# Neighbourhood attention with the softmax scale applied to the probabilities and the tile pipeline one tile deeper

## What is computed

```python
s_nb = q @ k_band.T * scale + bias          # window of 8 x 16 positions, the rest masked
s_ctx = q @ k_ctx.T * scale
p = softmax(concatenate([s_nb, s_ctx]))     # one softmax over both
o = p[:, :n_band] @ v_band + p[:, n_band:] @ v_ctx
```

## Time and profile before

| | us |
|---|---|
| median of 3 runs (lowest to highest) | 4434.53 (4432.39 to 4434.57) |
| the profiled execution's own time | 4424.82 |
| its span, first to last instruction | 4422.8 |
| mean granted TensorE clock | 0.939 of full |
| PE busy over the span | 3919.2 (89%) |
| attention groups, first scores to last output | 259.3 to 1040.6 |

### The profile page before, as it was taken

The page is one execution under the profiler, slowest core; times in us unless marked ns, Lnnn a source line. Parts: engine busy times, 40 slices in busy tenths (PEclk is TensorE's granted clock), DMA queues, the critical chain, the costliest instruction groups (busy, mean ns, idle before and its releaser), DMA issues. The chain is left out here.

```text
span 4422.8 us, 55661 instructions
## 1 busy us (share of the span) xinstructions
PE 3919.2 (89%) x23164; PEld 2962.6 (67%) x23164; DVE 1172.5 (27%) x3113; ACT 799.4 (18%) x1768; POOL 497.6 (11%) x497
## 2 busy tenths in 40 slices
PE   5599999988949999999966999999988699999994
PEld 0266666664537789999844666666645589997873
DVE  2312222221221011111125555555533201111114
ACT  0123333331100000000012333333321000000001
POOL 0210000001420000000024111111013200000002
PEclk9799999998969999999988999999988799999997
DMA  9670000010155446778952000000102645579995
GB/s 371 185 305 24 19 24 19 19 48 25 43 180 171 134 151 214 247 261 277 311 194 65 14 16 15 15 15 15 44 15 78 206 162 194 193 249 310 311 308 171
DMA packets 469098, 621.06 MB, mean 140 GB/s; under 512 B 27136, under 2 KB 346128, under 8 KB 468728
## 3 DMA queue, kind: packets, MB, share of 16 engines
q1 hardware_dynamic: 440312, 521.58, 35.9%
q0 software_dynamic: 22240, 73.58, 4.6%
q10 hardware_dynamic: 6312, 22.45, 1.3%
HBM read 550.54 MB, written 67.40 MB: 140 GB/s over the span
## 5 line engine op out<-in xcount | busy, mean ns | idle before, releaser
L1610 PE MATMUL ps<-item_xT,expert_ring 128*128 128x128 f32 (+9 forms) x8192 | 1169.4, 306 | 1.1 <-DVE item_xT L1687 1.1
L1610 PEld LDWEIGHTS ps<-item_xT,expert_ring 128*128 128x128 f32 x8192 | 1115.6, 192 | 57.2 <-issue 5.7
L1643 PE MATMUL ps<-item_aT,expert_ring 128*128 128x144 f32 (+8 forms) x2304 | 409.1, 333 | 0.0
L1643 PEld LDWEIGHTS ps<-item_aT,expert_ring 128*128 128x128 f32 x2304 | 359.7, 193 | 25.3 <-issue 2.0
L1694 DVE TENSOR_TENSOR item_aT<-item_silu,ps 128x128 f32<-128x128 f32 (+9 forms) x256 | 83.8, 327 | 1069.2 <-ACT item_silu L1664 1069.2
L1664 ACT ACTIVATE item_silu<-ps 128x128 f32<-128x128 f32 (+9 forms) x256 | 79.1, 309 | 1314.9 <-PE ps L1610 1314.9
L683 PE MATMUL ps<-hT,w_group 128*128 128x512 f32 (+1 forms) x704 | 270.2, 527 | 0.4 <-PEq L301 0.4
L383 PE MATMUL ps<-hT,oT 128*128 128x512 f32 x576 | 254.5, 602 | 1.4 <-PEq L917 0.7
L1009 PE MATMUL ps<-hT,w_group 128*128 128x512 f32 (+1 forms) x576 | 232.4, 546 | 0.4 <-PEq L301 0.4
L1560 POOL DMA_INDIRECT gathered<-h_rows,slot_idx x55 | 52.6, 956 | 1531.2 <-PE ps L1593 1520.3
L1705 DVE COPY item_y<-ps 128x512 f32<-128x512 f32 (+3 forms) x106 | 69.0, 684 | 573.9 <-PE ps L1623 397.0
(11 more groups left out here) (207 smaller groups left out, 4223.5 us busy)
## 6 DMA issues: line engine op xcount, KB each, us to landing
expert_ring<-in_expert_w_gate SPq DMA_DIRECT2D x128, 1024.0 KB, 5.1
expert_ring<-in_expert_w_up SPq DMA_DIRECT2D x128, 1024.0 KB, 8.0
expert_ring<-in_expert_w_down SPq DMA_DIRECT2D x64, 2048.0 KB, 7.7
mod_ring<-in_mod_w SPq DMA_DIRECT2D x24, 2048.0 KB, 14.0
slot_out<-rows POOLq DMA_DIRECT2D x7, 4096.0 KB, 46.3
w_group<-in_w_qkv SPq DMA_DIRECT2D x48, 512.0 KB, 3.7
slot_out<-item_y ACTq DMA_DIRECT2D x35, 512.0 KB, 7.5
h_rows<-hr SPq DMA_DIRECT2D x18, 512.0 KB, 2.6
```

Of the source, the lines that this page charges most:

```text
L1610: m = nc.tensor.matmul(gub(j, b, w), ring[:, b // 2, k, w * 256 + (b % 2) * P:w * 256 + (b % 2 + 1) * P], xT[:, k, 0:C], start=k == 0, sto ...
L1643: m = nc.tensor.matmul(yb(j, d), ring[:, 4 + d // 4, f, (d % 4) * P:(d % 4 + 1) * P], aT[:, f, 0:C], start=f == 0, stop=f == FB - 1)
```

## The change

The probabilities are now scaled by the inverse sums on DVE before they are transposed (`normalised`), in place of a diagonal, a matmul, a copy and a product behind `values`. The scores of a tile are issued two tiles ahead, not one; they wait (`s_pre`) until DVE has read the scores of the tile before out of the score banks. A projection chunk is issued in one piece at the end of a tile's turn. The transposes of the fifth block go to bank 6, beside the values, where they wait for `s_oT`.

```diff
-                FIFTH = bank(4, 0, 2 * P).rearrange("p (h n) -> p h n", h=2)
+                FIFTH = bank(6, P, 3 * P).rearrange("p (h n) -> p h n", h=2)
                 O = bank(6, 0, P)
-                INV = bank(6, P, 2 * P)
...
                     def scores(g, par, i):
                         t = order[i]
                         if i == 0:
                             pe.wait_ge(s_qk, g * NQK + NQK)
+
+                        pe.wait_ge(s_pre, g * 2 * NS + 2 * i)
...
-                    def transposes(g, i):
+                    def transposes(g, i, first=False):
                         n = len(near_keys(order[i]))
-                        if i == 0:
-                            pe.wait_ge(s_v, g * 3 + 3)
                         for h in range(2):
-                            pe.wait_ge(s_exp, g * 2 * NS + 2 * i + h + 1)
+                            pe.wait_ge(s_nm, g * 2 * NS + 2 * i + h + 1)
...
+                        if n > 4:
+                            if not first or i:
+
+                                pe.wait_ge(s_oT, g * NS + i)
...
                     def group(g, par, first=False, last=False):
                         for i in range(NS):
-                            if i + 1 < NS:
-                                scores(g, par, i + 1)
+                            values(g, par, i, first)
+                            if i + 2 < NS:
+                                scores(g, par, i + 2)
                             elif not last:
-                                scores(g + 1, 1 - par, 0)
-                            fifths(g, i)
-                            inverse_rows(g, i, first)
-                            if i < NM and not last:
-                                project(g + 1, i, 0)
-                            values(g, par, i)
-                            if i < NM and not last:
-                                project(g + 1, i, 1)
+                                scores(g + 1, 1 - par, i + 2 - NS)
                             if i + 1 < NS:
                                 transposes(g, i + 1)
                             elif not last:
                                 transposes(g + 1, 0)
+                            if i < NM and not last:
+                                project(g + 1, i)
...
                     scores(0, 0, 0)
-                    transposes(0, 0)
+                    transposes(0, 0, True)
+                    scores(0, 0, 1)
...
                         for h in range(2):
-                            nc.vector.tensor_scalar(dg[:, h, :], ident, rl[:, h:h + 1], None, ALU.mult).then_inc(s_dg, 1)
+                            nc.vector.tensor_scalar(pb[:, i % 2, h, 0:w], pb[:, i % 2, h, 0:w], rl[:, h:h + 1], None, ALU.mult).then_inc(s_nm, 1)
...
-                        nc.vector.tensor_tensor(oT[:, g * NTOK + order[i] * P:g * NTOK + (order[i] + 1) * P], O, inv, ALU.mult).then_inc(s_oT, 1)
+                        nc.vector.tensor_copy(oT[:, g * NTOK + order[i] * P:g * NTOK + (order[i] + 1) * P], O).then_inc(s_oT, 1)
```

More of the change, by code:

```diff
@@ L561, in neighbourhood @@
                 rl = sb(c, "na_suminv", [P, 2])
-                dg = rows[:, 1, HALF:HALF + 2 * P].rearrange("p (h n) -> p h n", h=2)
-                inv = rows[:, 1, HALF + 2 * P:HALF + 3 * P]
                 raw = sb(c, "bias_raw", [P, 2, NEAR])
@@ L571, in neighbourhood @@
                 s_z, s_cleared = sem(c, "zeros_set"), sem(c, "slots_cleared")
-                s_mm, s_qk, s_v, s_S, s_pre, s_max, s_exp, s_T, s_pT, s_rl, s_dg, s_bc, s_inv, s_o, s_oT, s_raw, s_tab = (
+                s_mm, s_qk, s_v, s_S, s_pre, s_max, s_exp, s_rl, s_nm, s_T, s_pT, s_o, s_oT, s_raw, s_tab = (
                     sem(c, n) for n in ("na_projected", "na_qk_taken", "na_v_taken", "na_scores", "na_biased",
-                                        "na_max", "na_exp", "na_transposed", "na_probsT_ready", "na_inverse", "na_diag_ready", "na_inverse_psum", "na_inverse_taken",
+                                        "na_max", "na_exp", "na_inverse", "na_normed", "na_transposed", "na_probsT_ready",
                                         "na_pv", "na_outT", "na_bias_in", "na_bias_table"))
@@ L694, in tiles, with project @@
                         return m
-                    def project(g, n, part):
+                    def project(g, n):
                         kind, c0, w = chunks[n]
[L699 to L708, removed]
+                        if n % 3 == 0:
+                            pe.wait_ge(w_in["qkv".index(kind)], (g + 1) * 16)
+                        if n == 0:
+                            pe.wait_ge(s_v, g * 3)
+                        elif n <= NQK:
+                            pe.wait_ge(s_qk, g * NQK + n)
+                        else:
+                            pe.wait_ge(s_v, g * 3 + n - NQK)
                         if kind == "v":
-                            m = tiles(PROJ, chunks[n], range(w // 2) if part == 0 else range(w // 2, w))
+                            m = tiles(PROJ, chunks[n], range(w))
                         else:
-                            m = some(PROJ, chunks[n], range(KD // 2) if part == 0 else range(KD // 2, KD))
-                        if part:
-                            m.then_inc(s_mm, 1)
+                            m = some(PROJ, chunks[n], range(KD))
+                        m.then_inc(s_mm, 1)
                     def scores(g, par, i):
@@ L736, in transposes @@
                             m.then_inc(s_T, 1)
-                    def fifths(g, i):
-                        if rounds(i) > 2:
-                            pe.wait_ge(s_pT, g * NR + r0[i] + 1)
+                        if n > 4:
+                            if not first or i:
+                                pe.wait_ge(s_oT, g * NS + i)
                             for h in range(2):
@@ L744, in fifths, with values @@
                             m.then_inc(s_T, 1)
-                    def inverse_rows(g, i, first):
-                        pe.wait_ge(s_dg, g * 2 * NS + 2 * i + 2)
+                    def values(g, par, i, first):
+                        if i == 0:
+                            pe.wait_ge(s_v, g * 3 + 3)
+                        pe.wait_ge(s_pT, g * NR + r0[i + 1])
                         if not first or i:
                             pe.wait_ge(s_oT, g * NS + i)
[L751 to L758, removed]
                         ks = near_keys(order[i])
@@ L822, in biased, with normalised @@
                         nc.vector.tensor_scalar(nmx[:, :], mx[:, :], -1.0, None, ALU.mult).then_inc(s_max, 1)
-                    def inverse(g, i):
+                    def normalised(g, i):
+                        w = len(near_keys(order[i])) * P
                         dve.wait_ge(s_exp, g * 2 * NS + 2 * i + 2)
@@ L828, in inverse @@
                         for h in range(2):
-                            nc.vector.tensor_scalar(dg[:, h, :], ident, rl[:, h:h + 1], None, ALU.mult).then_inc(s_dg, 1)
+                            nc.vector.tensor_scalar(pb[:, i % 2, h, 0:w], pb[:, i % 2, h, 0:w], rl[:, h:h + 1], None, ALU.mult).then_inc(s_nm, 1)
                     def output(g, i):
                         dve.wait_ge(s_o, g * NS + i + 1)
-                        dve.wait_ge(s_inv, g * NS + i + 1)
-                        nc.vector.tensor_tensor(oT[:, g * NTOK + order[i] * P:g * NTOK + (order[i] + 1) * P], O, inv, ALU.mult).then_inc(s_oT, 1)
+                        nc.vector.tensor_copy(oT[:, g * NTOK + order[i] * P:g * NTOK + (order[i] + 1) * P], O).then_inc(s_oT, 1)
                     def group(g, par, last=False):
                         for i in range(NS):
[L838 to L841, removed]
                             output(g, i)
[L843 to L846, removed]
+                            if i + 2 < NS or not last:
+                                biased(g + (i + 2) // NS, (i + 2) % NS)
+                                normalised(g + (i + 2) // NS, (i + 2) % NS)
                             if NQK <= i < NM and not last:
@@ L851, in _ @@
                         take_values(0, 0, n, ahead_bank[n])
-                    biased(0, 0)
-                    inverse(0, 0)
+                    for i in range(2):
+                        biased(0, i)
+                        normalised(0, i)
                     for g in range(GROUPS):
@@ L882, in take_probs @@
                             nc.scalar.activation(pT[:, :, 4 * P:5 * P], FIFTH, ACT.Copy).then_inc(s_pT, 1)
-                    def take_inverse(g, i):
-                        act.wait_ge(s_bc, g * NS + i + 1)
-                        nc.scalar.activation(inv, INV, ACT.Copy).then_inc(s_inv, 1)
                     def group(g, par, last=False):
                         for i in range(NS):
[L890 to L897, removed]
                             if i + 1 < NS:
@@ L901, in group @@
                                 take_probs(g + 1, 0)
+                            if i + 2 < NS:
+                                exps(g, i + 2)
```

(6 more changed lines are left out.)

## The result

| | before | after | ratio, 95% interval |
|---|---|---|---|
| median of 4 runs, us | 4433.46 | 4302.34 | 0.9703, 0.9686 to 0.972 |
| lowest to highest | 4430.11 to 4434.57 | 4296.61 to 4303.54 | |
| the profiled execution | 4424.82 | 4301.71 | |

131.1 us less, where 103.7 were forecast; the forecast of 4330.8 is 28 too high, and its range, 4312 to 4352, ended above the result. The two profiled executions differ by 123.1.

The account below looks back on a forecast made before the run. PE's instruction stream bounds the projecting groups, the softmax chain through DVE and ACT the last. Gains of 6.4 (group 0), 6 x 10.8 and 32.5 (last group) sum to 103.7: 4434.5 - 103.7 = 4330.8 us, range 4312 to 4352.

Parts of the forecast that it names:

- Undivided chunks: PE in projecting groups: joining the two halves of a chunk saves 0.11 us for each of 9 chunks, 1.0 a group.
- terms 1 and 2: PE in projecting groups: removing `inverse_rows` saves 0.37 us a tile, 3.7 a group; joining chunk halves 0.11 a chunk, 1.0.
- I take 0.82: DVE's new scaling: 0.82 us for one instruction of 640 columns, between bounds of 284 and 1186 ns.
- 5.46: Last group: DVE sets a beat of 5.46 us for a tile of 5 blocks.
- third rival: DVE's scaling at two elements a clock: 0.49 us in place of 0.82, 8 us less, 4323; chance 0.10.
- The edge: Group's edge, no chunk before tile 0's values: PE loses 0.86 us for ACT's copies and 0.5 for scaled heads, 1.4 in all.
- allowance for half rate: Last group: 1.5 us allowed for PE records at half rate, taking its gain from 34.0 to 32.5.
- gain mostly absent: Projecting groups: joins between record shapes keep PE busy and the edge still stalls; 70 us less, 4365; chance 0.10.
- half-clock rival: Last group and edges: PE runs at half rate in short gaps, 16 us lost, 4347; chance 0.13.

Follow-up runs that it names:

- run 1: The kernel before, with only the projection chunk issued whole, in front of `values`: 4409.16 us, ratio 0.9951 to the kernel before.
- run 6: The changed kernel with each chunk in two halves, one before and one behind the transposes: 4305.03 us, ratio 0.9716 to the kernel before.
- run 7: The changed kernel with PE's order transposes, half chunk, fifth transposes, half chunk: 4302.87 us, ratio 0.9706 to the kernel before.
- run 8: The changed kernel with each chunk's first half between `values` and scores, second behind the transposes: 4316.75 us, ratio 0.9742 to the kernel before.
- run 5: The changed kernel with the scaling as a product of two tensors, the inverse sums broadcast: 4315.32 us, ratio 0.9735 to the kernel before.
- run 2: The changed kernel with scores issued one tile ahead, DVE's scaling queued behind `output`: 4439.6 us, ratio 1.0019 to the kernel before.
- run 3: The changed kernel with scores one tile ahead and DVE's `output` moved behind the scaling: 4372.72 us, ratio 0.9872 to the kernel before.
- scores_first: The changed kernel with tile 1's scores issued before tile 0's transposes in front of the groups: 4299.62 us, ratio 0.9700 to the kernel before.
- both improvements: The changed kernel with tile 1's scores first in front and four v chunks, the last at tile 9: 4291.65 us, ratio 0.9683 to the kernel before.

## Why the prediction was wrong

The order of events was right step by step: no wait of `values` for ACT in the projecting tiles, one at the edge, DVE setting the beat of the last group, full clock. Sizes were wrong, all in one direction.

1. **"Undivided chunks: 1.0 a group."** This term failed, in size and in reason, and with it the fifth transposes, whose gain I had put at nothing. Runs 1 and 6 show that joining or dividing is worth 0.4 a group. What I had read from 3.63 against 3.54 as a join was one change more in the use of the array. The old order changes it six times a tile (transposes, scores, fifths, inverse rows, chunk, values, chunk), the new one three times. A tile with five key blocks saves 0.75 us of PE time where my terms 1 and 2 gave 0.48, 0.27 more; there are six of these in a group, and the three with v chunks, which have no fifth block, save some 0.15 more. That is 2.1 a group, and 14 to 15 us in seven groups. That the changes are the cause is shown for the chunk by runs 1, 7 and 8, and for the fifth transposes by run 7 (0.22 there, 0.37 in the earlier trace rows). What PE does in such a change no run shows.
2. **"I take 0.82, since at 128 columns this instruction shows no advantage."** Wrong choice between bounds: 0.55 was measured. Run 5 puts its worth at 7.9 us of the stage, 3.2 of them in the last group, where my 5.46 became 4.90. My third rival, scaling at twice the speed, had 8 us for it and a chance of 0.10. It rests on a rule that I set aside: the Trainium skill (VectorE: DVE Perf Modes, the perf-mode tier table) lets an fp32 tensor_scalar from SBUF to SBUF run at twice the speed of one element a clock. The trace agrees: 0.52 ns a column, half of L804's 1.04. By the page's figures 640 columns would be an estimated 0.49 us; the trace has 0.55.
3. **The edge.** I counted 1.4 us lost, 0.86 for ACT's copies and 0.5 for the scaled heads. The waits of after are 0.80 for the copies and none for the heads, which is (2) again.
4. **The last group's allowance for half rate**, 1.5 us, was not needed: granted clock 1.00.

(1), (2) and (4) come to some 24 for the 22.6 that the stage gave beyond my sum. The total gave 131.1 - 103.7 = 27.4 beyond it. The other 4.8 lie outside the stage: before's profiled execution was 8.6 below its median and after's 0.6, which adds 8.0, and outside the stage after's profiled execution lost 3.2. I subtracted a gain read from one execution from the median of others, which is sound only to that spread; before's runs went from 4420.6 to 4444.4 in these comparisons.

The rival "gain mostly absent" named the right place, the joins between shapes, with the wrong sign: the removed changes of shape were worth more than I had counted. The half-clock rival didn't occur: the last group has a granted clock of 1.00, the groups before it 0.99.

## To carry to other kernels

A short instruction can't tell two speeds apart: before pricing a wide one from a narrow row, ask what either speed would give at the narrow width, and keep both if the row fits both. Count the changes between matmuls that use the whole array, half of its rows or half of its columns as work of their own (0.1 to 0.2 us each here), and put like beside like. In a fixed order, look at what stands behind each waiting instruction: one line moved on DVE was worth 67 us (runs 2 and 3), half of what the whole change gave.

## What the runs showed beside that

PE's loop over pairs of groups costs time at its turn. In the changed kernel the group in which it turns back takes 89.3 us in place of 85.6:

```profile
619.32 1.31 PE L750 MATMUL ps<-rows,na_V 128*64 128x128 f32 x20 [2.90 <-issue]
620.57 2.34 PE L720 MATMUL ps<-na_kT,na_qT 64*128 64x384 f32 x12
...
622.84 1.73 PE L730 MATMUL ps<-con,na_probs 128*128 128x128 f32 x8
```

PE stands 2.90 us where it waits 0.80 in other groups, and the records behind run at half rate (2.34 for 1.36, 1.73 for 1.09). With the loop written out all groups take 84.7. The two parts can be told apart: in `scores_first` PE stood 2.74 us and the records behind ran at full rate, and that group took 87.5 for 85.6; with both improvements it stood 1.65, again with full rate behind, and the group took 86.5 for 84.7. So the standing costs 1.7 to 1.9 us in these kernels, and the rest of the 3.7 is half rate, which comes in some traces and not in others. The kernel before had 101.9 for 98.8 to 99.5, with the whole chunk 97.0 for 96.2 to 97.0. Whether the lost time is the branch or the supply of instructions behind it stays open.
